# Suffix sums and gate sums of a two-block transformer kernel: fp32 matmuls replaced by pairs of fp32r matmuls on split data

## The chip, the cores and the metric

The kernel runs on one core of one Trainium2 chip. The time is the device time in microseconds of one execution. Three runs of the kernel before gave 1718.21, 1718.66 and 1719.46 us, median 1718.66.

## What is computed

Two transformer blocks over 256 tokens of width 2048, all data fp32. The first block mixes tokens in three ways (12 heads of windowed attention with a sink, 4 heads of gated linear attention, 8 heads of stick-breaking attention), then has a squared-ReLU MLP of width 8192. The second has grouped-query attention in a window, a pooling branch, gates and merges. The change touches two sums of the first block:

```
# stick-breaking attention: sum over later keys
log_1m_beta = where(strict, log_sigmoid(-z), 0)
between     = cumsum(log_1m_beta, reverse=True) - log_1m_beta
w           = where(strict, exp(log_sigmoid(z) + between), 0)
out         = w @ v

# gated linear attention, chunks of 64 tokens
log_gate = max(log_sigmoid(gate_pre) / 16, -1)
b        = cumsum(log_gate)            # within a chunk
q_dec, k_inv, k_end = q * exp(b), k * exp(-b), k * exp(b_last - b)
```

Both are written as products with constant 128x128 matrices of zeros and ones (`mats`): C_SUFFIX (a >= b) and C_ONES for the suffix sums, C_TRI and C_REV (within a chunk, up to and after a token) for the gate sums.

## The kernel before

Weights stream from memory in pieces of 256 rows by 512 columns; one piece is a slot (or sub). For each slot SyncE loads `raw`, ScalarE copies it to `w_hi` (fp32r, a shorter format, which rounds), VectorE writes `w_lo = raw - w_hi` (line 1259), and TensorE does three products per operand pair: hi by hi, hi by lo, lo by hi. In the first phase, P1, that is 12 matmuls a slot (`gemm`, line 653), with the activations `X_pair` as the stationary operand and the weights as the moving one. ScalarE and VectorE make the halves three slots ahead of TensorE; four pieces of halves and eight of raw weights fit on chip. Blocks of columns take eight slots; the block in slots 48 to 55 has 272 columns, the others of this stretch 512.

Everything else is in named stages, each at a slot of its phase (the STAGES list, `stage(phase, slot, name, P=, A=, D=, G=)`, which counts the semaphore steps that it takes on TensorE, ScalarE, VectorE and GpSimd). Each engine walks through the slots in order (`walk`, line 500): at slot s TensorE does the matmuls of s, ScalarE and VectorE the halves of s + 3, and after that each does its part of the stages of slot s. Before its part of a stage an engine calls `enter` (line 492), which waits until all engines have done all stages that stand before it in the list:

```python
def enter(eng, name, turn=None):
    phase, before_, _ = BASE[name]
    for e in "PADG":
        if before_[e]:
            n = before_[e]
            eng.wait_ge(SIDE[e], ...)
```

The stick-breaking heads go in two groups of four, 0 and 1. sb_Z: scores on TensorE, two copies to SBUF on ScalarE. sb_P: exponential and logarithm on ScalarE. sb_Q (line 1401): VectorE makes `soft`, 128 x 1536, and masks it. sb_S (line 877): five fp32 matmuls of the matrices with `soft` (three of 512 columns, two of 256); then VectorE subtracts and masks (lines 1413 to 1420). sb_W: exponential on ScalarE, line 1135. sb_V: 12 matmuls with 64 columns of values, copied out by VectorE, line 1424. The stages in0 to in10 move a finished block of products out of PSUM on ScalarE (line 1097), and free its bank for the second block behind it.

The gated attention: gla_A and gla_B make the gate's argument, gla_K (VectorE) the log gates `lg`, 128 x 2 x 384. gla_C: four fp32 matmuls of C_TRI and C_REV with `lg` (384 columns each, lines 914 and 915), eight small fp32 ones (line 919), then ScalarE's exponentials. swa_N takes mean squares of the windowed attention's result on ScalarE, with a root on GpSimd. gla_D (VectorE, last line 1435) multiplies q and k, gla_E transposes them on TensorE (line 623), and so on to gla_O. In the trace each fp32 matmul shows as two instructions.

The stage "vectors" at slot 9 makes some small constants on VectorE.

Of the kernel before, what the change touches and what calls it, by code (L numbers as in the profile page):

```python
# [27 lines left out]
P = 128  # L28
D_MODEL = 2048
TOK = 256  # L30
NT = TOK // P
KC = D_MODEL // P
NW = 512
# [31 lines left out]
V_MIX, V_MLP, V_PRE, V_GAIN, V_C, V_POOL, V_FIN, V_MER, V_COLS = 0, 16, 32, 48, 64, 80, 88, 104, 136  # L65

C_ID, C_TRI, C_REV, C_SUFFIX, C_STRICT, C_NEG, C_ONES, C_CHUNK = range(8)


def constants():  # L70
# [104 lines left out]
def stage(phase, slot, name, P=0, A=0, D=0, G=0):  # L175
    STAGES.append((phase, slot, name, dict(P=P, A=A, D=D, G=G)))
# [25 lines left out]
stage("P1", 43, "sb_Z0", P=1, A=2)  # L202
stage("P1", 44, "sb_P0", A=2)
stage("P1", 46, "sb_Q0", D=2)
stage("P1", 49, "sb_S0", P=1, D=2)
stage("P1", 50, "in5", A=1)
stage("P1", 52, "sb_W0", A=1)
stage("P1", 54, "sb_V0", P=1, D=1)
stage("P1", 55, "sb_Z1", P=1, A=2)
stage("P1", 56, "sb_P1", A=2)  # L210
stage("P1", 57, "gla_ones", G=1)
stage("P1", 58, "sb_Q1", D=2)
stage("P1", 60, "in6", A=1)
stage("P1", 61, "sb_S1", P=1, D=2)
stage("P1", 63, "sb_W1", A=1)
stage("P1", 64, "in7", A=1)
stage("P1", 65, "sb_V1", P=1, D=1)
stage("P1", 66, "gla_A", P=1, A=1)
stage("P1", 66, "sb_N", A=2, G=2)
stage("P1", 68, "gla_B", P=1, A=3)  # L220
stage("P1", 69, "sb_M", D=1)
stage("P1", 70, "gla_K", D=2)
stage("P1", 71, "in8", A=1)
stage("P1", 73, "gla_C", P=1, A=1)
stage("P1", 75, "swa_N", A=2, G=2)
stage("P1", 75, "gla_D", D=1)
stage("P1", 77, "gla_E", P=1, A=1, D=1)
# [106 lines left out]
def done(e, name, turn=None):  # L334
    return step(e, name, BASE[name][2][e], turn)


def program(nc, t, out):
    f32, f32r = mybir.dt.float32, mybir.dt.float32r
    ACT = mybir.ActivationFunctionType  # L340
    AX = mybir.AxisListType
    ctx = ExitStack()
    with ctx:
# [9 lines left out]
        def put(name, at, shape, dt=f32):  # L353
            size = (4 * int(np.prod(shape[1:])) + 31) // 32 * 32
            assert at + size <= room - 64, (name, at, size, room)
            return nc.alloc_sbuf_tensor_at(name, shape, dt, offset=base + at), at + size

        raw, at = put("raw", 0, [P, RAW, SUB, NW])
        w_hi, at = put("w_hi", at, [P, SPLIT, SUB, NW], f32r)
        w_lo, at = put("w_lo", at, [P, SPLIT, SUB, NW], f32r)  # L360
        x, at = put("x_res", at, [P, NT, D_MODEL])
        X_AT = at
        x_pair, at = put("X_pair", at, [P, KC, 2, TOK], f32r)
        x_hi, x_lo = x_pair[:, :, 0, :], x_pair[:, :, 1, :]
        mats, at = put("mats", at, [P, 8, P])
        vecs, at = put("vecs_sb", at, [P, V_COLS])
        stat, at = put("stat", at, [P, 96])
        small, at = put("small", at, [P, 96])
        half, at = put("minus_half", at, [P, 8])
        cs, at = put("c_silu", at, [P, KC])  # L370
        ada_v, at = put("ada_v", at, [P, 2, KC])
        pre_g, at = put("pre_gain", at, [P, KC])
        sinks, at = put("sinks", at, [P, SWA_HEADS + Q_HEADS2])
        nsinks, at = put("nsinks", at, [P, SWA_HEADS + Q_HEADS2])
        AR = at
        Y_AT = (room - 64 - 32 * KB) // 32 * 32
        y_pair, _ = put("Y_pair", Y_AT, [P, KC, 2, TOK], f32r)
# [3 lines left out]
        swa, at = put("swa", AR, [P, NT, SWA_END])  # L381
        sbp, at = put("sbp", at, [P, NT, 3 * SB_W])
        gla, at = put("gla", at, [P, NT, SB_AT - SWA_END])
        M1_AT = at
        bias1, at = put("bias1", M1_AT, [P, SWA_HEADS, TOK])
        HT_AT = at
        heads_T, at = put("heads_T", HT_AT, [HD, 16, TOK])
        PR_AT = at
        probs, at = put("probs", PR_AT, [P, 1536])
        probs_T, at = put("probs_T", at, [P, 1536])  # L390
        soft, at = put("soft", at, [P, 1536])
        assert at <= room - 64, (at, room)
        onehot, _ = put("onehot_sb", PR_AT, [BUCKET_ROWS, 2, TAB])
        rel, _ = put("rel_sb", PR_AT + 4 * KB, [BUCKET_ROWS, SWA_HEADS + Q_HEADS2])
        tab, _ = put("tab_sb", PR_AT + 8 * KB, [SWA_HEADS, 2, TAB])

        GW = GLA_HEADS * GLA_DK
        GV = GLA_HEADS * GLA_DV
        lg, at = put("log_gate", M1_AT, [P, NT, GW])
        e_dec, at = put("e_dec", at, [P, NT, GW])  # L400
        e_inv, at = put("e_inv", at, [P, NT, GW])
        e_end, at = put("e_end", at, [P, NT, GW])
        assert at <= HT_AT
        qd_T, at = put("qd_T", HT_AT, [GLA_DK, NT, GLA_HEADS, P])
        ki_T, at = put("ki_T", at, [GLA_DK, NT, GLA_HEADS, P])
        sc_T, at = put("sc_T", at, [P, NT, GLA_HEADS, P])
        blr_T, at = put("blr_T", at, [GLA_RANK + 1, TOK])
        gw, at = put("gw_sb", at, [GLA_RANK + 1, GW])
        dec, at = put("decay", at, [GLA_DK, GLA_HEADS, 2 * NT])
        assert at <= PR_AT  # L410
        state, at = put("state", PR_AT, [GLA_DK, 3, GLA_HEADS, GLA_DV])
        k_inv, at = put("k_inv", PR_AT + 9 * KB, [P, NT, GW])

        ada_w, at = put("ada_w", AR, [P, 2, ADA_W])
        hid, at = put("hid", at, [P, NT, NW])
        x_nf, at = put("x_nf", at, [P, NT, NW])
        norm_f, at = put("norm_f", at, [P, D_MODEL])
        acc, at = put("ada_acc", at, [P, ADA_W])
        acc_T, at = put("ada_acc_T", at, [P, ADA_W])
        at = max(at, AR + 48 * KB)  # L420
        ada_sum, at = put("ada_sum", at, [P, QUARTERS * ADA_W // GRP])
        gate_T, _ = put("gate_T", at, [KC, P])
        b_ada, at = put("b_ada", at, [ADA_ROWS, P])
        post, at = put("post_gain", at, [KC, P])
        gate_v, at = put("gate_v", at, [P, KC])
        row, at = put("gate_row", at, [P, D_MODEL])
        assert at <= Y_AT, (at, Y_AT)

        y_n, _ = put("y_n", X_AT, [P, NT, D_MODEL])
        tmp_T, _ = put("tmp_T", X_AT + 16 * KB, [P, 4, NW])  # L430
# [7 lines left out]
        ya, at = put("ya", AR, [P, Q_HEADS2, TOK])  # L438
        v2, at = put("v2", at, [P, NT, KV_HEADS2 * P])
        probs2_T, at = put("probs2_T", AR + 12 * KB, [P, 4, 2, P])  # L440
        ga, at = put("ga", at, [P, 8, TOK])
        yp, _ = put("yp", at, [P, 8, TOK])
        u, at = put("u", at, [P, 8, PAD + TOK + PAD])
        gp, at = put("gp", at, [P, 8, TOK])
        sums, at = put("window_sums", at, [P, 2, 2, PAD + TOK + PAD])
        assert at <= AR + 48 * KB
        pool_edge, _ = put("pool_edge", AR + 10 * KB, [P, 4, 2, PAD])

        sig, at = put("sig", AR, [P, 2, 4, TOK])
        br, _ = put("br", at, [P, 4, TOK])  # L450
        m_hi, at = put("M_hi", AR + 16 * KB, [P, KC, TOK], f32r)
        m_lo, at = put("M_lo", at, [P, KC, TOK], f32r)
        o_sb, _ = put("o_sb", AR, [P, NT, D_MODEL])
        sq, _ = put("sq", X_AT, [P, NT, NW])
# [166 lines left out]
        def _(pe):  # L621
# [169 lines left out]
            def stages(name, i):  # L791
# [85 lines left out]
                elif name[:4] == "sb_S":  # L877

                    pe.wait_ge(const_in, 48)
                    for a in range(2):  # L880
                        nc.tensor.matmul(S[:, a, :], mats[:, C_SUFFIX, :], soft[:, NW * a:NW * (a + 1)],
                                         start=True, stop=False)
                        late = S[:, a, :].rearrange("p (h q) -> p h q", h=2)[:, :, P:TOK]
                        nc.tensor.matmul(late, mats[:, C_ONES, :], soft[:, 2 * NW + TOK * a:2 * NW + TOK * (a + 1)]
                                         .rearrange("p (h q) -> p h q", h=2), start=False, stop=True)
                    nc.tensor.matmul(S[:, 2, :], mats[:, C_SUFFIX, :], soft[:, 2 * NW:3 * NW],
                                     start=True, stop=True).then_inc(pe_side, 1)
                elif name[:4] == "sb_V":
                    for k in range(4):
                        h = 4 * int(name[-1]) + k  # L890
# [20 lines left out]
                elif name == "gla_C":  # L911

                    for tt in range(NT):
                        nc.tensor.matmul(S[:, tt, 0:GW], mats[:, C_TRI, :], lg[:, tt, :], start=True, stop=True)
                        nc.tensor.matmul(S[:, 2 + tt, 0:GW], mats[:, C_REV, :], lg[:, tt, :], start=True, stop=True)
                    for h in range(GLA_HEADS):
                        for tt in range(NT):
                            c_ = GW + 4 * h + 2 * tt
# [81 lines left out]
        def _(act):  # L1000
# [38 lines left out]
            def stages(name, i):  # L1039
# [89 lines left out]
                elif name[:4] == "sb_P":  # L1129

                    nc.scalar.activation(probs_T[:, :], probs_T[:, :], ACT.Exp, scale=-1.0).then_inc(act_side, 1)
                    act.wait_ge(act_side, step("A", name, 1))
                    nc.scalar.activation(soft[:, :], probs_T[:, :], ACT.Ln, bias=1.0).then_inc(act_side, 1)
                elif name[:4] == "sb_W":
                    nc.scalar.activation(probs_T[:, :], probs[:, :], ACT.Exp).then_inc(act_side, 1)
                elif name == "gla_A":
# [117 lines left out]
        def _(dve):  # L1254
# [68 lines left out]
            def stages(name, i):  # L1323
# [86 lines left out]
                elif name[:4] == "sb_S":  # L1410
# [7 lines left out]
                    b = probs[:, 1024:1536].rearrange("p (h q) -> p h q", h=4)  # L1418
                    nc.vector.tensor_tensor(a, a, neg, ALU.add)
                    nc.vector.tensor_tensor(b, b, neg, ALU.add).then_inc(dve_side, 1)  # L1420
                elif name[:4] == "sb_V":
                    dve.wait_ge(pe_side, done("P", name))
                    c = 4 * HD * int(name[-1])
# [102 lines left out]
                elif name == "vectors":  # L1526

                    dve.wait_ge(const_in, 48)
                    nc.vector.tensor_scalar(nsinks[:, :], sinks[:, :], -1.0, None, ALU.mult)
                    nc.vector.tensor_tensor(pre_g[:, :], vecs[:, V_PRE:V_PRE + KC], vecs[:, V_FIN:V_FIN + KC],  # L1530
                                            ALU.mult).then_inc(dve_side, 1)
# [234 lines left out]
```

## Time and profile before

| | us | share | instructions |
|---|---|---|---|
| profiled execution | 1718.24 | | |
| its span | 1716.4 | 100% | 27560 |
| TensorE matmul | 1696.1 | 99% | 10425 |
| TensorE weight load | 1507.0 | 88% | 10425 |
| VectorE | 1104.2 | 64% | 1115 |
| ScalarE | 824.6 | 48% | 1072 |
| GpSimd | 55.0 | 3% | 53 |

The time is the execution's own; the span goes from its first to its last instruction. Shares are busy time over the span. Matmuls are pipelined, so their shown durations overlap: the distance between starts says what one costs in a stream. The mean granted TensorE clock was 0.998 of full speed.

### The profile page before, as it was taken

The page shows a single profiled execution, that of the slowest core. Times are in us where ns is not written, and L with a number is a line of the kernel's source. Part 1 is how long each engine was busy: PE and PEld are TensorE (multiplying, and loading weights), DVE is VectorE, ACT ScalarE, POOL GpSimd, SP SyncE. Part 2 cuts the span into 40 slices and gives each one's busy share as a digit, 9 for nine tenths or more (in the row PEclk, how much of TensorE's full clock was granted, in tenths as well). Part 3 has the DMA queues.
Part 4 walks back from the last instruction along what each step waited for, and adds up shares of the span by engine and source line. Part 5 has one row for each costly group of instructions (what it writes and reads, how often), then busy time and mean ns, then how long its engine had stood idle before and what let it go on. Part 6 is the DMA issues. An engine that isn't in the chain of part 4 may idle for free.

```text
span 1716.4 us, 27560 instructions
## 1 busy us (share of the span) xinstructions
PE 1696.1 (99%) x10425; PEld 1507.0 (88%) x10425; DVE 1104.2 (64%) x1115; ACT 824.6 (48%) x1072; POOL 55.0 (3%) x53
## 2 busy tenths in 40 slices
PE   9999999999999999999999999999999999999998
PEld 6888888789998999889988998799989988888886
DVE  4544545555777677777777777765565566757654
ACT  6455554544444544454444444444434444444443
POOL 1000000000000000000000000000000001101100
PEclk9999999999999999999999999999999999999999
DMA  8642644466777777777777787656455656565662
GB/s 305 192 147 63 199 148 149 140 210 222 278 271 264 252 250 273 261 258 276 253 249 265 268 283 260 227 172 202 156 163 169 189 180 195 183 190 177 197 207 87
DMA packets 170689, 361.59 MB, mean 211 GB/s; under 512 B 10907, under 2 KB 15579, under 8 KB 170336
## 3 DMA queue, kind: packets, MB, share of 16 engines
q1 hardware_dynamic: 168272, 352.24, 61.9%
q0 software_dynamic: 2032, 7.56, 1.3%
q8 instruction: 73, 1.20, 0.3%
q10 hardware_dynamic: 288, 0.39, 0.1%
q14 instruction: 24, 0.20, 0.0%
HBM read 358.00 MB, written 2.15 MB: 210 GB/s over the span
## 4 chain that ended last, share of the span: by engine, by line
PE 83%; DVE 1%; issue 0%; DVEq 0%; POOL 0%; ACT 0%; ACTq 0%
PE G L636 32%; PE G L653 30%; PE S L667 5%; PE G L667 5%; PE G L670 3%; PE S L670 3%; PE S L653 3%; PE S L623 1%; PE G L642 1%; PE S L986 0%; PE S L979 0%; PE S L966 0%; PE S L940 0%; PE S L951 0%; PE S L955 0%
## 5 line engine op out<-in xcount | busy, mean ns | idle before, releaser
L1259 DVE TENSOR_TENSOR w_lo<-raw,w_hi 128x1024 fp32r<-128x1024 f32 (+2 forms) x576 | 708.1, 1245 | 467.6 <-ACT w_hi L1009 466.2
L1009 ACT ACTIVATE w_hi<-raw 128x1024 fp32r<-128x1024 f32 (+2 forms) x576 | 594.8, 1046 | 586.9 <-PE G L653 230.6
L653 PE MATMUL G<-w_hi,X_pair 128*128 128x512 f32 (+2 forms) x1984 | 607.7, 385 | 2.1 <-DVE w_lo L1259 1.3
L636 PE MATMUL G<-Y_pair,w_hi 128*128 128x256 f32 x3136 | 554.7, 280 | 0.0
L636 PEld LDWEIGHTS G<-Y_pair,w_hi 128*128 128x128 f32 x3136 | 478.4, 188 | 2.8 <-issue 1.9
L653 PEld LDWEIGHTS G<-w_hi,X_pair 128*128 128x128 f32 x1984 | 368.8, 188 | 79.3 <-issue 5.7
L636 PE MATMUL G<-Y_pair,w_lo 128*128 128x256 f32 x1568 | 437.1, 279 | 0.0
L653 PE MATMUL G<-w_lo,X_pair 128*128 128x512 f32 (+2 forms) x992 | 379.6, 383 | 0.0
L636 PEld LDWEIGHTS G<-Y_pair,w_lo 128*128 128x128 f32 x1568 | 294.8, 188 | 0.0
L653 PEld LDWEIGHTS G<-w_lo,X_pair 128*128 128x128 f32 x992 | 186.5, 188 | 35.6 <-issue 0.5
L1272 DVE SCALAR_TENSOR_TENSOR ada_acc<-ada_w,c_silu,ada_acc 128x768 f32<-128x768 f32 x120 | 121.3, 1011 | 0.0
L667 PE MATMUL S<-Y_pair,w_hi 128*128 128x512 f32 x256 | 88.9, 390 | 0.0
L667 PE MATMUL G<-Y_pair,w_hi 128*128 128x512 f32 x256 | 88.9, 390 | 0.0
L670 PE MATMUL S<-Y_pair,w_lo 128*128 128x256 f32 x256 | 72.2, 282 | 0.0
L670 PE MATMUL G<-Y_pair,w_lo 128*128 128x256 f32 x256 | 72.2, 282 | 0.0
L667 PEld LDWEIGHTS G<-Y_pair,w_hi 128*128 128x128 f32 x256 | 48.0, 188 | 10.1
L667 PEld LDWEIGHTS S<-Y_pair,w_hi 128*128 128x128 f32 x256 | 48.0, 188 | 10.1
L670 PEld LDWEIGHTS S<-Y_pair,w_lo 128*128 128x128 f32 x256 | 48.4, 189 | 0.0
L670 PEld LDWEIGHTS G<-Y_pair,w_lo 128*128 128x128 f32 x256 | 48.4, 189 | 0.0
L667 PE MATMUL S<-X_pair,w_hi 128*128 128x512 f32 x128 | 44.6, 391 | 0.0
L667 PE MATMUL G<-X_pair,w_hi 128*128 128x512 f32 x128 | 44.5, 391 | 0.0
L1192 ACT ACTIVATE S<-x_res 128x512 f32<-128x512 f32 x32 | 19.3, 603 | 43.9 <-DVE x_res L1505 43.4
(292 smaller groups left out, 1269.5 us busy)
## 6 DMA issues: line engine op xcount, KB each, us to landing
raw<-in_w_in SPq DMA_DIRECT2D x144, 512.0 KB, 4.4
raw<-in_w_mlp_in SPq DMA_DIRECT2D x128, 512.0 KB, 5.3
raw<-in_w_mlp_out SPq DMA_DIRECT2D x128, 512.0 KB, 6.5
ada_w<-in_w_ada SPq DMA_DIRECT2D x64, 768.0 KB, 4.8
raw<-in_w_out SPq DMA_DIRECT2D x64, 512.0 KB, 4.3
raw<-in_w_merge SPq DMA_DIRECT2D x64, 512.0 KB, 4.1
raw<-in_w_branch_attn SPq DMA_DIRECT2D x16, 512.0 KB, 4.3
raw<-in_w_branch_pool SPq DMA_DIRECT2D x16, 512.0 KB, 5.7
```

The costliest lines, as they stand in the source:

```text
L623: return nc.tensor.transpose(out_, in_, ident)
L636: ins = nc.tensor.matmul(G[:, bank, j // 2, TOK * (j % 2):TOK * (j % 2 + 1)], w[:, s % SPLIT, c, cut], a[:, c0 + c, :], start=first and c ...
L642: ins = nc.tensor.matmul(G[:, bank, 1, TOK * tt:TOK * (tt + 1)], a[:, c0 + c, P * tt:P * (tt + 1)], w[:, s % SPLIT, c, P * turned:NW], sta ...
L653: ins = nc.tensor.matmul(token_bank(bank, tt)[:, 0:n], a[:, c0 + c, tok], w[:, s % SPLIT, c, 0:n], start=first and c == 0 and k == 0, stop ...
L667: nc.tensor.matmul(bank, w_hi[:, s % SPLIT, c, cut], both[:, c0 + c, :, :].rearrange("p a q -> p (a q)"), start=first and c == 0, stop=Fal ...
L670: ins = nc.tensor.matmul(bank[:, 0:TOK], w_lo[:, s % SPLIT, c, cut], both[:, c0 + c, 0, :], start=False, stop=last and c == SUB - 1, skip_ ...
L1009: nc.scalar.activation(w_hi[:, s % SPLIT, :, 0:n], raw[:, k, :, 0:n], ACT.Copy).then_inc(hi_ready, 1)
L1192: nc.scalar.activation(junk, src, ACT.Square, scale=D_MODEL ** -0.5, accum_out=stat[:, c:c + 1]).then_inc(act_side, 1)
L1259: nc.vector.tensor_tensor(w_lo[:, s % SPLIT, :, 0:n], raw[:, k, :, 0:n], w_hi[:, s % SPLIT, :, 0:n], ALU.subtract).then_inc(lo_ready, 1)
L1272: nc.vector.scalar_tensor_tensor(a, w, cs[:, v:v + 1], a, ALU.mult, ALU.add).then_inc(ada_free, 1)
```

## The change

The data of the sums are split as the weights are: a half `hi` (rounded copy on ScalarE) and a half `lo = data - hi` (VectorE), both fp32r. The matrices are copied once to fp32r, in which zeros and ones are exact. Each fp32 matmul becomes two fp32r matmuls that add into the same bank, the matrix with `hi` and with `lo`. The two new kinds of stages, sb_H0 and sb_H1 behind sb_Q and gla_H behind gla_K, make the halves. `soft_hi` lies on `probs_T`, `soft_lo` on `soft`, `lg_hi` and `lg_lo` on the places of `e_dec` and `e_inv`, all free at that time. Most stages between slots 49 and 73 move one slot later, and in5 now stands before sb_S0 in the list. The eight small matmuls of gla_C stay fp32.

```diff
-stage("P1", 49, "sb_S0", P=1, D=2)
+stage("P1", 47, "sb_H0", A=1, D=1)
 stage("P1", 50, "in5", A=1)
-stage("P1", 52, "sb_W0", A=1)
-stage("P1", 54, "sb_V0", P=1, D=1)
+stage("P1", 50, "sb_S0", P=1, D=2)
+stage("P1", 53, "sb_W0", A=1)
+stage("P1", 55, "sb_V0", P=1, D=1)
 stage("P1", 55, "sb_Z1", P=1, A=2)
 stage("P1", 56, "sb_P1", A=2)
 stage("P1", 57, "gla_ones", G=1)
 stage("P1", 58, "sb_Q1", D=2)
+stage("P1", 59, "sb_H1", A=1, D=1)
 stage("P1", 60, "in6", A=1)
-stage("P1", 61, "sb_S1", P=1, D=2)
-stage("P1", 63, "sb_W1", A=1)
+stage("P1", 62, "sb_S1", P=1, D=2)
 stage("P1", 64, "in7", A=1)
-stage("P1", 65, "sb_V1", P=1, D=1)
+stage("P1", 64, "sb_W1", A=1)
+stage("P1", 66, "sb_V1", P=1, D=1)
 stage("P1", 66, "gla_A", P=1, A=1)
 stage("P1", 66, "sb_N", A=2, G=2)
 stage("P1", 68, "gla_B", P=1, A=3)
 stage("P1", 69, "sb_M", D=1)
 stage("P1", 70, "gla_K", D=2)
 stage("P1", 71, "in8", A=1)
-stage("P1", 73, "gla_C", P=1, A=1)
+stage("P1", 72, "gla_H", A=1, D=1)
+stage("P1", 74, "gla_C", P=1, A=1)
...
                 elif name[:4] == "sb_S":
...
-                        nc.tensor.matmul(S[:, a, :], mats[:, C_SUFFIX, :], soft[:, NW * a:NW * (a + 1)],
-                                         start=True, stop=False)
                         late = S[:, a, :].rearrange("p (h q) -> p h q", h=2)[:, :, P:TOK]
-                        nc.tensor.matmul(late, mats[:, C_ONES, :], soft[:, 2 * NW + TOK * a:2 * NW + TOK * (a + 1)]
-                                         .rearrange("p (h q) -> p h q", h=2), start=False, stop=True)
...
+                        for half_ in (soft_hi, soft_lo):
+                            nc.tensor.matmul(S[:, a, :], sum_m[:, M_SUFFIX, :], half_[:, NW * a:NW * (a + 1)],
+                                             start=half_ is soft_hi, stop=False, skip_group_check=True)
+                        for half_ in (soft_hi, soft_lo):
+                            nc.tensor.matmul(late, sum_m[:, M_ONES, :], half_[:, 2 * NW + TOK * a:2 * NW + TOK * (a + 1)]
+                                             .rearrange("p (h q) -> p h q", h=2), start=False, stop=half_ is soft_lo,
+                                             skip_group_check=True)
...
                 elif name == "gla_C":
...
-                        nc.tensor.matmul(S[:, tt, 0:GW], mats[:, C_TRI, :], lg[:, tt, :], start=True, stop=True)
-                        nc.tensor.matmul(S[:, 2 + tt, 0:GW], mats[:, C_REV, :], lg[:, tt, :], start=True, stop=True)
+                        for bank, m in ((tt, M_TRI), (2 + tt, M_REV)):
+                            for half_ in (lg_hi, lg_lo):
+                                nc.tensor.matmul(S[:, bank, 0:GW], sum_m[:, m, :], half_[:, tt, :],
+                                                 start=half_ is lg_hi, stop=half_ is lg_lo, skip_group_check=True)
...
+                elif name[:4] == "sb_H":
+                    act.wait_ge(dve_side, done("D", name.replace("H", "Q")))
+                    nc.scalar.activation(soft_hi[:, :], soft[:, :], ACT.Copy).then_inc(act_side, 1)
+                elif name == "gla_H":
+                    act.wait_ge(dve_side, done("D", "gla_K"))
+                    nc.scalar.activation(lg_hi[:, :, :], lg[:, :, :], ACT.Copy).then_inc(act_side, 1)
...
+                elif name[:4] == "sb_H":
+                    dve.wait_ge(act_side, done("A", name))
+                    nc.vector.tensor_tensor(soft_lo[:, :], soft[:, :], soft_hi[:, :], ALU.subtract).then_inc(dve_side, 1)
+                elif name == "gla_H":
+                    dve.wait_ge(act_side, done("A", name))
+                    nc.vector.tensor_tensor(lg_lo[:, :, :], lg[:, :, :], lg_hi[:, :, :], ALU.subtract).then_inc(dve_side, 1)
...
                 elif name == "vectors":
 
                     dve.wait_ge(const_in, 48)
+                    nc.vector.tensor_copy(sum_m[:, M_TRI:M_SUFFIX + 1, :], mats[:, C_TRI:C_SUFFIX + 1, :])
+                    nc.vector.tensor_copy(sum_m[:, M_ONES, :], mats[:, C_ONES, :])
```

## Rows read from the trace of the kernel before

**Rows 1.** Waits of TensorE, whole span: us in total, times, longest

```profile
PE S L623 <- DVE y_n L1347: 2.0, 1, 2.0
```

**Rows 2.** Chain that ended last, 120 to 310 us: start, us, what

```profile
265.69 1.92 PE S L623 x16
267.62 5.48 PE G L653 x24
```

**Rows 3.** TensorE's timeline around sb_S0: start, us, operation, [idle before <- releaser]

```profile
173.36 1.02 PE L881 MATMUL S<-soft,mats 128*128 128x512 f32 x2
...
176.92 0.28 PE L653 MATMUL G<-w_lo,X_pair 128*128 128x272 f32 x1
...
177.30 0.29 PE L653 MATMUL G<-w_lo,X_pair 128*128 128x272 f32 x1
...
185.59 0.41 PE L893 MATMUL S<-sbp,probs_T 128*128 128x64 f32 x2 [0.86 <-issue]
...
188.27 0.37 PE L653 MATMUL G<-w_hi,X_pair 128*128 128x272 f32 x1
...
189.94 0.70 PE L872 MATMUL S<-heads_T 64*128 64x256 f32 x2
```

**Rows 4.** ScalarE's timeline, 155 to 225 us

```profile
167.34 1.73 ACT L1009 ACTIVATE w_hi<-raw 128x544 fp32r<-128x544 f32 x3
...
180.34 1.27 ACT L1097 ACTIVATE sbp<-G,stat 128x512 f32<-128x512 f32 x2 [6.07 <-DVE probs L1420]
...
182.71 1.28 ACT L1135 ACT_TABLE_LOAD   x1
184.01 1.49 ACT L1135 ACTIVATE probs_T<-probs 128x1536 f32<-128x1536 f32 x1
```

**Rows 5.** VectorE's timeline, 155 to 225 us

```profile
171.69 0.68 DVE L1409 TENSOR_TENSOR soft<-soft,mats 128x512 f32<-128x512 f32 x1
172.29 1.99 DVE L1259 TENSOR_TENSOR w_lo<-raw,w_hi 128x544 fp32r<-128x544 f32 x3
177.09 1.75 DVE L1413 TENSOR_TENSOR probs<-probs,S 128x1536 f32<-128x1536 f32 x1 [2.81 <-PE S L886]
```

**Rows 6.** TensorE's timeline around sb_S1 and sb_V1

```profile
209.22 1.02 PE L881 MATMUL S<-soft,mats 128*128 128x512 f32 x2
...
226.18 0.47 PE L653 MATMUL G<-w_hi,X_pair 128*128 128x512 f32 x1
```

**Rows 7.** ScalarE's timeline, in6

```profile
207.36 0.87 ACT L1097 ACTIVATE gla<-G,stat 128x272 f32<-128x272 f32 x2 [2.27 <-DVE soft L1409]
```

**Rows 8.** VectorE's timeline, end of sb_Q1 and sb_V1

```profile
206.51 0.69 DVE L1409 TENSOR_TENSOR soft<-soft,mats 128x512 f32<-128x512 f32 x1
...
226.50 0.69 DVE L1424 COPY sbp<-S 128x512 f32<-128x512 f32 x1 [2.66 <-PE S L897]
```

**Rows 9.** TensorE's timeline, gla_C to gla_E

```profile
250.03 0.81 PE L914 MATMUL S<-log_gate,mats 128*128 128x384 f32 x2
...
252.61 1.44 PE L919 MATMUL S<-mats,log_gate 128*96 128x2 f32 x16
253.92 0.49 PE L653 MATMUL G<-w_hi,X_pair 128*128 128x512 f32 x1
...
265.69 0.28 PE L623 MATMUL S<-mats,gla 128*96 128x128 f32 x1 [0.59 <-DVE gla L1435]
```

**Rows 10.** ScalarE's timeline, 225 to 275 us

```profile
247.25 2.00 ACT L1009 ACTIVATE w_hi<-raw 128x1024 fp32r<-128x1024 f32 x2
...
257.61 2.02 ACT L1009 ACTIVATE w_hi<-raw 128x1024 fp32r<-128x1024 f32 x2
```

**Rows 11.** Windows: us, busy (x instructions) of PE, PEld, DVE, ACT, POOL, granted clock, DMA

```profile
1116.00:1118.00 2.00, 0.63 (x2) 0.00 (x0) 0.59 (x4) 0.05 (x1) 1.03 (x1) 1.00 0.00 0
1118.00:1124.00 6.00, 5.33 (x31) 5.04 (x32) 5.09 (x14) 4.24 (x9) 0.00 (x0) 0.72 0.01 3
```

**Rows 12.** TensorE's timeline, stage h2_T0

```profile
1118.67 3.53 PE L623 MATMUL S<-mats,y_n 128*128 128x128 f32 x16 [2.04 <-DVE y_n L1347]
```

More of the change, by code:

```diff
@@ L67 @@
 C_ID, C_TRI, C_REV, C_SUFFIX, C_STRICT, C_NEG, C_ONES, C_CHUNK = range(8)
+M_TRI, M_REV, M_SUFFIX, M_ONES = range(4)
 def constants():
@@ L389, in program @@
         probs, at = put("probs", PR_AT, [P, 1536])
+        soft_hi, _ = put("soft_hi", at, [P, 1536], f32r)
         probs_T, at = put("probs_T", at, [P, 1536])
+        soft_lo, _ = put("soft_lo", at, [P, 1536], f32r)
         soft, at = put("soft", at, [P, 1536])
+        sum_m, at = put("sum_mats", at, [P, 4, P], f32r)
         assert at <= room - 64, (at, room)
@@ L399, in program @@
         lg, at = put("log_gate", M1_AT, [P, NT, GW])
+        lg_hi, _ = put("log_gate_hi", at, [P, NT, GW], f32r)
         e_dec, at = put("e_dec", at, [P, NT, GW])
+        lg_lo, _ = put("log_gate_lo", at, [P, NT, GW], f32r)
         e_inv, at = put("e_inv", at, [P, NT, GW])
@@ L880, in stages @@
                     for a in range(2):
-                        nc.tensor.matmul(S[:, a, :], mats[:, C_SUFFIX, :], soft[:, NW * a:NW * (a + 1)],
-                                         start=True, stop=False)
                         late = S[:, a, :].rearrange("p (h q) -> p h q", h=2)[:, :, P:TOK]
-                        nc.tensor.matmul(late, mats[:, C_ONES, :], soft[:, 2 * NW + TOK * a:2 * NW + TOK * (a + 1)]
-                                         .rearrange("p (h q) -> p h q", h=2), start=False, stop=True)
-                    nc.tensor.matmul(S[:, 2, :], mats[:, C_SUFFIX, :], soft[:, 2 * NW:3 * NW],
-                                     start=True, stop=True).then_inc(pe_side, 1)
+                        for half_ in (soft_hi, soft_lo):
[5 more added lines that the diff above has]
+                                             skip_group_check=True)
+                    for half_ in (soft_hi, soft_lo):
+                        ins = nc.tensor.matmul(S[:, 2, :], sum_m[:, M_SUFFIX, :], half_[:, 2 * NW:3 * NW],
+                                               start=half_ is soft_hi, stop=half_ is soft_lo, skip_group_check=True)
+                    ins.then_inc(pe_side, 1)
                 elif name[:4] == "sb_V":
```

## The prediction

> **What bounds the kernel now.** I first read who TensorE waits for over the whole span [rows 1]. The longest entry is 2.0 us of some 1716, so TensorE's own queue sets the time, and an edit counts by what it does there: the work it removes, and the idle time it makes or ends. Near the change another engine leads at one place: VectorE's stage gla_D ends and releases TensorE's gla_E, 16 transposes [rows 9]; from there the chain that ended last stays on TensorE [rows 2]. Then I read the timelines around the three changed sums: TensorE, ScalarE and VectorE for the first suffix sum [rows 3 to 5], the second [rows 6 to 8], the gate sums [rows 9, 10]. A slot is one step of weight work, 12 matmuls; the narrow block has 272 columns in slots 48 to 55.
>
> **Price of the two forms on TensorE.** Starts are what counts, not the durations shown, which overlap. One fp32 suffix stage holds TensorE from 173.36 to 176.92 minus one ordinary pitch, 3.43 us [rows 3]. In the new form it is six matmuls of 512 columns and four of 256. The weight matmuls have exactly that form: 24 in 5.48 us, so 0.228 each at 512 columns and 2.74 a slot [rows 2]; at 272 columns three in 0.38, so 0.125 [rows 3], and I take 256 at the same. Sum 6 x 0.228 + 4 x 0.125 = 1.87 us: 1.56 saved per stage, two stages. The gate sums take 252.61 - 250.03 = 2.58 us [rows 9]. New: eight of 384 columns; between 0.125 and 0.228 in proportion that is 0.173, so 1.38 us: 1.20 saved. In all 4.3 us of TensorE work go. Bounds: above, no saving at all (the operands of 0/1 stationary and split moving data are not in the trace together); below, 384 columns at the 272 price, another 0.4. I take the pitch of the weight matmuls, whose form is the same.
>
> **Price of the halves.** Every stage starts with a wait for all stages before it in the list, on all engines. So the stages are one serial chain, and a new stage lengthens it. sb_H copies 1536 columns on ScalarE; sb_W does as many from the same memory in 1.49 us [rows 4]. It then subtracts 1536 on VectorE, 1.75 as for L1413 [rows 5]. gla_H has half the columns. The copies of the matrices in stage "vectors" (512 columns in all) cost less than L1413's 1.75 on VectorE; the three slots that w_lo is made ahead, 8 us, hide them, and without that cover they would cost at most 1.75. I take nothing. No DMA moves, and SP's loads wait for w_lo seven slots back, so they are not reached.
>
> **First suffix sum.** VectorE ends sb_Q0 at 171.69 + 0.68 = 172.37 [rows 5]. ScalarE, which waits in sb_H0 instead of going on with slot 51's weights, copies from 172.5 to 174.0. VectorE subtracts to 175.8. ScalarE makes the three narrow copies of slots 51 to 53 meanwhile (1.73, [rows 4]), which fit before 175.8. But in5 now stands ahead of sb_S0 in the list, and so sb_S0 waits for it too: 175.8 + 0.16 (207.20 to 207.36 in [rows 7, 8]) + 1.27 [rows 4] = 177.25, and with 0.15 to get TensorE going 177.4. TensorE now does slot 50 first (12 x 0.125 = 1.5; its w_lo, the first of the three in [rows 5], is there at 173.0, before 173.36): it is ready at 173.36 + 1.50 = 174.86. **New idle: 2.5 us.** The sum ends at 179.27. Slots 51 to 55 (7.5) bring TensorE to 186.8. The chain: VectorE's part of sb_S0 took from 177.09 to about 180.2, 3.1 us [rows 4, 5], so it ends at 182.6; ScalarE then does slot 56's wide copy to 183.5, a table load of 1.28 and the exponential 1.49 [rows 4], done 186.3. So sb_V0 is not waited for, and the old idle before it (0.86 shown, 1.0 by pitches, plus 0.27 in slot 54 for w_lo) goes. But sb_V0 and sb_Z1 now stand in one slot with no weight work between. sb_Z1 waits for VectorE's copy of sb_V0's result: 0.32 after the last matmul until it starts, 0.69 for it, 0.2 back [rows 6, 8]. **New idle: 1.2 us.** sb_V0 takes 188.27 - 185.59 = 2.68 [rows 3], so sb_Z1 starts at 186.8 + 2.7 + 1.2 = 190.7, against 189.94 [rows 3]: 0.75 later than before, although 1.56 of work is gone.
>
> **Second suffix sum.** Everything is 0.75 later. sb_Q1 ends at 206.51 + 0.69 + 0.75 = 207.95 [rows 8]; copy to 209.6, subtraction to 211.4, in6 (0.87, [rows 7]) to 212.4. TensorE, with slot 62 now first, arrives at 209.22 + 0.75 + 2.74 = 212.7 [rows 6]: ready, with 0.1 to spare. 1.56 gained. Then the same neighbourhood again: sb_V1 and gla_A share slot 66, where slot 66's matmuls stood between them: 1.2 idle, less 0.1 for one switch of form fewer. Shift now 0.75 - 1.56 + 1.2 - 0.1 = 0.3 later.
>
> **Gate sums.** gla_H goes between in8 and gla_C. ScalarE's copies for slots 75 and 76 ran from 247.25 in 2.00 [rows 10]; the half copy (under 1.49) and the subtraction (under 1.75) with waits end before 252, and TensorE comes from slot 74 only at 250.03 + 0.3 + 2.74 = 253.07. Hidden; if not, it would cost one for one. gla_C ends at 253.07 + 1.38 + 1.31 (the 16 small ones, unchanged) = 255.76, 1.84 later than 253.92 [rows 9]. Behind it hangs the chain to gla_E: exponentials, swa_N, POOL's root, gla_D, gla_E. Of it one wide copy drops out (slot 77's, now ahead of gla_C; the two took 2.02 at 257.61, [rows 10]): -1.0. So gla_E starts 0.85 later, at 266.5. TensorE has only three slots between instead of four: 255.76 + 8.22 = 263.98. **New idle: 2.55 us, where 0.8 was (0.59 shown).** The 1.20 saved here disappears in it. What is late next is this chain, and behind gla_E nothing changes.
>
> **Sum.** +0.85 us on the profiled execution's 1718.24 (span 1716.4 and 1.84 around it): 1719.1. The median of the runs is 0.42 above that execution: 1719.5. A difference under 0.2%, 3.4 us, can't be told from none here.
>
> **Clock.** At 1116 to 1118 TensorE was idle for most of the time; its wait was 2.04 us, and when it came back with transposes, the granted clock fell: mean 0.72 over 1118 to 1124, which is (1 - 0.72) x 6 / 0.5 = 3.4 us at 0.5, 1.2 GHz [rows 11]. The 16 transposes there took 3.53 us [rows 12] against 1.92 for the 16 of gla_E [rows 2]. Price of a fall: half of 3.4, 1.7 us. The Trainium skill, "TensorE: Matmul & The Clock Gate", section "HAM oscillation — how this bites in real kernels", says that bursts of matmuls parted by waits come back at half the clock and pay beyond the wait. The trace agrees at this one place. [...] The waits of 0.86 and 0.59 us [rows 3, 9] left the clock at full speed, and by them alone it would be 1719.5.
>
> **Rivals.**
> - Half clock after the new waits. Place: the idle of 2.5 before sb_S0 and of 2.55 before gla_E, the latter followed by transposes as in rows 12. For: both are longer than 2.04. Against: dense weight work stands right ahead of both and behind the first, while at 1116 the work around was thin. One fall: 1719.5 + 1.7 = 1721.2. Both: 1722.9, slower than the bound of 1722.1. It decides from the second fall on.
> - The halves and in5 are out of the way in time, and the work saved is kept: 4.3 and the old idles of 1.27 and 0.8 give 1718.66 - 6.4 = 1712.3. Against it: even with both halves free, sb_S0 would wait for in5 until 175.8 or so. With that, half of the way: 1717.5, no change.
> - The form doesn't do what it says: fp32 speed remains. Then 3.1 of the two suffix stages comes back and of the gates 1.2: 1723.8. Against: L653 is that form.
>
> **Chances.** Forecast 0.50 (its own range 1718.3 to 1720.7, from latencies of 0.1 to 0.3 in four waits). One fall of the clock 0.20, both 0.13. Waits smaller than I count 0.12, half of it past 3.4 us. No gain from the form 0.05. Faster: 0.06. Slower: 0.13 + 0.05, less 0.02 for cases that come out milder: 0.16. Within: 0.78. Range 1716.5 to 1722.9: it takes in both falls and leaves out the full gain and the form without gain.
>
> **What would show it.** Fp32r pairs at S at 0.228 spacing; TensorE idle ahead of sb_S0 by 2.5 with in5 as the last to end; 1.2 before sb_Z1 and before gla_A, both on VectorE's copy; no idle before sb_V0; 2.5 before gla_E, whose start is at 266 to 267. Wrong: gla_E before 265, clock below 1.00 between 170 and 275, or halves longer than 1.8 us.

## The result and the profile after

The changed kernel takes 1722.72 us in the median of 20 runs (1718.83 to 1727.54), the kernel before 1717.89 (1716.81 to 1719.46, 20 runs). The ratio is 1.0027, interval 1.0020 to 1.0033: slower by 4.8 us in the medians. The forecast was 1719.5 with a range of 1716.5 to 1722.9. The time is in the range, 0.2 us below its upper end, but the likeliest case was not what happened: a difference of less than 0.2% had 0.78, and the result is the slower case, which had 0.16. The spread is a finding of its own: 8.7 us between runs, where the kernel before has 2.7. It goes with the clock: the mean granted clock of a run falls from 0.999 in the fastest to 0.994 in the slowest, and 0.005 of 1720 us is 8.6 us.

The profiled execution took 1721.95 us, its span 1720.1 against 1716.4. The page:

```profile
PE 1693.1 (98%) x10425; PEld 1506.8 (88%) x10425; DVE 1109.0 (64%) x1120; ACT 828.1 (48%) x1075; POOL 55.0 (3%) x53
```

TensorE is 3.0 us less busy than before with as many instructions, and still the span is 3.7 longer. The waits of TensorE (us in total, times, longest) name where:

```profile
PE S L892 <- ACT sbp L1113: 2.4, 1, 2.4
PE S L632 <- DVE gla L1463: 2.4, 1, 2.4
PE S L632 <- DVE y_n L1369: 2.0, 1, 2.0
...
PE S L632 <- DVE sbp L1452: 1.1, 1, 1.1
PE S L881 <- DVE sbp L1452: 1.1, 1, 1.1
```

Three of these are new: sb_S0 waits for in5's copy (sbp, ScalarE), gla_A and sb_Z1 for VectorE's copies out of sb_V. A fourth, gla_E's wait for gla_D, was 0.59 before [rows 9]. The two short ones come from the list. Of the twenty stages between slots 49 and 73 only seven move; sb_Z1 and gla_A stay, so sb_V0 now shares slot 55 with sb_Z1, and sb_V1 shares slot 66 with gla_A, with no weight matmuls between. TensorE's timeline around sb_S0, to be held against [rows 3]:

```profile
174.66 0.28 PE L662 MATMUL G<-w_hi,X_pair 128*128 128x272 f32 x1
177.37 0.47 PE L892 MATMUL S<-soft_hi,sum_mats 128*128 128x512 f32 x1 [2.42 <-ACT sbp L1113]
177.68 0.40 PE L892 MATMUL S<-soft_lo,sum_mats 128*128 128x512 f32 x1
177.91 0.28 PE L895 MATMUL S<-soft_hi,sum_mats 128*128 128x256 f32 x1
...
179.30 0.29 PE L662 MATMUL G<-w_hi,X_pair 128*128 128x272 f32 x1
...
186.82 0.33 PE L907 MATMUL S<-sbp,probs_T 128*128 128x64 f32 x2
...
190.69 0.67 PE L881 MATMUL S<-heads_T 64*128 64x256 f32 x2 [1.08 <-DVE sbp L1452]
```

The pairs take 179.30 - 177.37 = 1.93 us where fp32 took 3.43, and sb_Z1 starts at 190.69 where it started at 189.94. Then the part that these rows don't show. The windows after it (us, busy of PE, PEld, DVE, ACT, POOL, granted clock, DMA):

```profile
186.00:190.00 4.00, 3.61 (x32) 3.47 (x31) 2.59 (x3) 2.32 (x3) 0.00 (x0) 1.00 0.87 304
190.00:192.00 2.00, 1.31 (x8) 1.23 (x9) 0.43 (x1) 0.00 (x0) 0.00 (x0) 1.00 0.87 291
192.00:194.00 2.00, 2.00 (x11) 1.74 (x9) 0.00 (x0) 0.00 (x0) 0.00 (x0) 0.66 0.59 211
194.00:196.00 2.00, 2.00 (x6) 1.49 (x5) 0.00 (x0) 1.61 (x2) 0.00 (x0) 0.50 0.00 0
196.00:198.00 2.00, 2.00 (x6) 1.53 (x5) 0.00 (x0) 2.00 (x2) 0.00 (x0) 0.50 0.00 0
198.00:200.00 2.00, 2.00 (x7) 1.52 (x7) 1.23 (x1) 1.98 (x3) 0.00 (x0) 0.63 0.00 0
200.00:202.00 2.00, 2.00 (x10) 1.65 (x9) 0.00 (x0) 1.99 (x2) 0.00 (x0) 1.00 0.71 199
```

The clock is at 0.50, 1.2 GHz, from about 193 to 199. The missing clock (what the stretch lacks to full speed) is (0.34 + 0.50 + 0.50 + 0.37) x 2 = 3.4 us. Before it stood sb_V0, 12 matmuls with 64 columns (thin ones, in what follows), 1.1 us of idle time, and sb_Z1 with 64 rows. Around it, across both waits of 2.4 us and the second short one, the clock stayed up:

```profile
170.00:190.00 20.00, 17.18 (x132) 16.52 (x131) 14.61 (x17) 11.33 (x13) 0.00 (x0) 1.00 0.71 237
202.00:280.00 78.00, 74.53 (x368) 61.97 (x367) 44.25 (x43) 42.93 (x53) 3.27 (x7) 1.00 0.48 156
```

The second suffix sum starts without a wait and takes 1.86 us:

```profile
215.83 0.39 PE L892 MATMUL S<-soft_hi,sum_mats 128*128 128x512 f32 x1
...
217.69 0.40 PE L662 MATMUL G<-w_hi,X_pair 128*128 128x512 f32 x1
```

The gates, beside [rows 9]:

```profile
256.23 0.34 PE L930 MATMUL S<-log_gate_hi,sum_mats 128*128 128x384 f32 x1
...
257.64 1.44 PE L935 MATMUL S<-mats,log_gate 128*96 128x2 f32 x16
258.95 0.47 PE L662 MATMUL G<-w_hi,X_pair 128*128 128x512 f32 x1
...
269.78 0.29 PE L632 MATMUL S<-mats,gla 128*96 128x128 f32 x1 [2.38 <-DVE gla L1463]
```

1.41 us for the pairs instead of 2.58. gla_E starts at 269.78 against 265.69: 4.1 later, 3.4 by the clock and 0.7 by the chain. Of that, 0.4 comes back near 1120 us, where this execution had no fall of the clock and [rows 11] had one: the 16 transposes take 2.14 us instead of 3.53, and a wait of 0.96 for Y_pair follows in their place.

```profile
1122.74 2.14 PE L632 MATMUL S<-mats,y_n 128*128 128x128 f32 x16 [2.04 <-DVE y_n L1369]
1125.85 0.50 PE L645 MATMUL G<-Y_pair,w_hi 128*128 128x256 f32 x2 [0.96 <-DVE Y_pair L1380]
```

### The profile page after: what moved, and what is told of

Its sections match the earlier page's. It is cut to its first block, busy times and chain, and to the rows that moved or that the text cites. A ratio compares the mean times of both kernels' runs of the same rounds, so it can differ in the third digit from the quotient of the medians.

```text
span 1720.1 us, 27580 instructions
## 1 busy us (share of the span) xinstructions
PE 1693.1 (98%) x10425; PEld 1506.8 (88%) x10425; DVE 1109.0 (64%) x1120; ACT 828.1 (48%) x1075; POOL 55.0 (3%) x53
## 4 chain that ended last, share of the span: by engine, by line
PE 83%; DVE 1%; issue 0%; ACT 0%; DVEq 0%; POOL 0%; ACTq 0%
PE G L645 32%; PE G L662 29%; PE S L676 5%; PE G L676 5%; PE G L679 3%; PE S L679 3%; PE S L662 3%; PE S L632 1%; PE G L651 1%; PE S L1002 0%; PE S L995 0%; PE S L982 0%; PE S L956 0%; PE S L967 0%; PE S L971 0%
```

## The experiments

Theory: the change saves 4.3 us of TensorE work; the chain of stages turns that into a net loss of about 0.9; and the rest is the clock, which falls behind stretches in which TensorE does little. Rivals: the waits or the pairs cost more by themselves; the halves are what costs; or the long waits, as the prediction had it, not the thin stretches, drop the clock.

### Filling the waits

The kernels do fp32 matmuls into a free bank before they enter the stage, and nobody reads the result: one before sb_Z1 and gla_A, two before sb_S0 and gla_E, there behind a wait for the bank's last reader. An entry of FILL has the stage, the number of matmuls, the bank and the stages to wait for:

```diff
+FILL = [('sb_Z1', 1, 0, []), ('gla_A', 1, 0, []), ('sb_S0', 2, 0, [('A', 'sb_P0'), ('D', 'sb_Q0')]), ('gla_E', 2, 3, [('A', 'gla_C')])]
...
+                for fill_name, fill_n, fill_bank, fill_after in FILL:
+                    if name == fill_name:
+                        for e_, st_ in fill_after:
+                            pe.wait_ge(SIDE[e_], done(e_, st_))
+                        for _ in range(fill_n):
+                            nc.tensor.matmul(S[:, fill_bank, :], mats[:, C_ONES, :],
+                                             mats[:, C_TRI:C_TRI + 4, :].rearrange("p a b -> p (a b)"), start=True, stop=True)
                 enter(pe, name, i)
```

The other kernels with filling have fewer entries in FILL. Their line numbers are up to 10 higher than in the changed kernel.

All four:

> The changed kernel with idle TensorE time filled: before it enters sb_S0 and gla_E it does two, before sb_Z1 and gla_A one fp32 matmul of 512 columns (0.85 us each) whose result nobody reads. Theory A (the new waits cost 0.85 us net, and the rest of the loss is the granted clock falling behind the thin stretches): no fall between 170 and 275 us, time 1718.7 to 1719.5, highest run within 2 us of the lowest. Rival B (the loss sits in the waits or in the new form itself, not in the clock): 1722.7 stays. Rival C (the filling comes late in its stage and delays it): up to 3 us more than 1722.7.

Measured 1719.34 (1718.33 to 1720.38, 11 runs), ratio to before 1.0009 (1.0000 to 1.0018). Adding work made the kernel 3.4 us faster, and the spread is 2.0 us. Theory A holds, B and C fall. By the medians the chain's price is some 1.3 us beside the 1717.99 of before. The profiled execution puts it at 0.76: gla_E starts at 266.45, where it started at 265.69.

```profile
266.45 1.92 PE S L633 x16
```

Only the two short waits behind sb_V:

> Filling only the two waits of 1.1 us before sb_Z1 and gla_A, one matmul each. Theory A1 (the falls start behind the thin stretches of 64-column matmuls and the wait after them, as in the profile, where the clock was 0.50 from 193 to 199 us): about 1719, as with all four filled. Rival A2 (the falls come from the two longer waits of 2.4 us before sb_S0 and gla_E): little changes, 1721 to 1723.

Measured 1719.56 (1718.11 to 1722.21, 11 runs), ratio 1.0014 (1.0005 to 1.0023). The median is that of all filled, but four of the 11 runs lie at 1720.7 or more, at a mean clock of 0.996 or 0.997. A1 for the most part. Where the clock fell in those four isn't shown; the open long waits are the likely place. In the profiled execution both stand open, and the clock is 1.00 from 170 to 275 us:

```profile
PE S L901 <- ACT sbp L1122: 2.4, 1, 2.4
PE S L633 <- DVE gla L1472: 2.4, 1, 2.4
```

There gla_E starts at 266.22, 0.53 later than before: this is the changed kernel's chain with the clock held.

Only the two long ones:

> The changed kernel with only the two waits of 2.4 us before sb_S0 and gla_E filled, two matmuls each; the thin stretches of sb_V and the waits behind them stay. With the two short waits filled instead, the time fell from 1722.7 to 1719.6 but single runs still reached 1722.2. Theory A1 (most falls start behind the thin stretches of sb_V): this kernel keeps them, median 1720.5 to 1722, single runs at 1723 or more. Rival A2 (the long waits are the main cause): 1719.5, as with all filled.

Measured 1723.15 (1718.38 to 1726.40, 10 runs), ratio 1.0029 (1.0019 to 1.0038): as slow as the changed kernel, and above the 1720.5 to 1722 expected. Eight of ten runs lie at 1721.6 or more, two at 1718.4. The windows of its profiled execution, with a fall behind each of the two sb_V:

```profile
186.00:196.00 10.00, 8.92 (x52) 7.84 (x51) 3.02 (x3) 4.47 (x5) 0.00 (x0) 0.84 0.61 211
...
228.00:238.00 10.00, 8.92 (x41) 7.10 (x40) 3.15 (x3) 3.83 (x7) 0.95 (x2) 0.83 0.41 134
```

The same windows with all four filled:

```profile
186.00:196.00 10.00, 9.83 (x61) 8.22 (x60) 3.02 (x3) 4.67 (x5) 0.00 (x0) 1.00 0.63 220
...
228.00:238.00 10.00, 9.83 (x40) 6.67 (x40) 3.05 (x3) 5.07 (x9) 0.95 (x2) 1.00 0.48 151
```

The stretch is the same but for 0.9 us of work in the middle. A2, which was the prediction's place for the fall, is refuted as the main cause. One thing stays open: the filling ends the idle time and puts a matmul of full width between two thin stretches, both at once, so these runs don't tell whether the wait or the thin work around it is what drops the clock.

### The slots alone

The kernel before with the changed list of slots, without sb_H and gla_H and with fp32 sums:

```diff
-stage("P1", 49, "sb_S0", P=1, D=2)
 stage("P1", 50, "in5", A=1)
+stage("P1", 50, "sb_S0", P=1, D=2)
...
-stage("P1", 73, "gla_C", P=1, A=1)
+stage("P1", 74, "gla_C", P=1, A=1)
```

> The kernel before with the changed kernel's list of slots, without the stages that make halves, sums in fp32 as before. By the chain: sb_S0 waits 0.7 us for in5, sb_Z1 and gla_A 1.2 each, gla_E starts 3.3 us later than in the kernel before. So 1721.2 with the clock held, and 2 to 4 us more where it falls: 1723 to 1725. Rival (the slots are free and the halves are what costs): 1718.

Measured 1725.94 (1725.20 to 1727.67, 5 runs), ratio 1.0049 (1.0035 to 1.0063). That is 0.9 above the expected 1723 to 1725; the rival's 1718 falls. The new order is slower than the whole change, without any pair or half in it. With the waits before sb_Z1, gla_A and gla_E filled as above:

> The kernel with only the slots changed (fp32 sums, no halves) and the waits before sb_Z1, gla_A and gla_E filled. Unfilled it took 1725.9, and its profile shows 10.2 us at half clock. If 3.3 us of its loss are the chain and the rest the clock, 1720.8 to 1721.5 here, with single runs close together. Rival (the waits themselves cost all of it): 1725.9 stays.

Measured 1721.25 (1720.58 to 1723.65, 11 runs), ratio 1.0019 (1.0010 to 1.0028). So the order costs 3.2 us by the chain (1718.04 before, beside it) and 4.7 by the clock. With the waits filled in both, the kernel with pairs takes 1719.34 and this one 1721.25: in these slots the pairs give back 1.9 of the 3.2, which leaves the 1.3 above. (This kernel has no filling before sb_S0, where its wait is 0.5.) The profile of the unfilled one has (1 - 0.75) x 10 + (1 - 0.76) x 4 + (1 - 0.88) x 14 = 5.1 us of missing clock in these windows:

```profile
186.00:196.00 10.00, 8.92 (x47) 7.81 (x47) 3.02 (x3) 2.77 (x4) 0.00 (x0) 0.75 0.62 213
196.00:200.00 4.00, 4.00 (x15) 3.22 (x14) 1.02 (x1) 4.00 (x4) 0.00 (x0) 0.76 0.00 0
...
266.00:280.00 14.00, 11.64 (x53) 9.65 (x52) 10.06 (x11) 6.78 (x10) 0.93 (x2) 0.88 0.39 120
```

The last of them holds the fall that the prediction expected: behind the wait of 2.4 us before gla_E and in its transposes. So that place can bring one; in the three other profiled executions with that wait open (the changed kernel, the short waits filled, the gate sums alone) it did not.

### The gate sums alone

The suffix sums and their slots as before, gla_H at 72 and gla_C at 74:

> Only the gate sums in the new form, with gla_H at 72 and gla_C at 74 as in the changed kernel; suffix sums and their slots as in the kernel before. By the chain behind gla_C: gla_E waits 2.5 us and starts 0.55 us later than in the kernel before, though 1.2 us of TensorE work is gone: 1718.4 with the clock held; a single long wait, followed by transposes, gives a fall in some runs: 1718.4 to 1719.5. Rival (the saved work is kept): 1716.8.

Measured 1718.07 (1717.72 to 1719.45, 11 runs), ratio 1.0003 (0.9994 to 1.0012), before beside it 1717.58. No difference can be told; the rival's 1716.8 lies below every run. The profile shows gla_E's wait of 2.4 us and the clock at 1.00 until the end:

```profile
PE S L630 <- DVE gla L1456: 2.4, 1, 2.4
```

```profile
260.00:280.00 20.00, 17.62 (x95) 14.85 (x94) 12.55 (x13) 9.90 (x14) 0.93 (x2) 1.00 0.43 132
```

By the median this long wait, with dense work ahead of it, costs nothing by the clock here. The 1.2 us of saved work show up nowhere.

### in5 behind sb_S0

```diff
-stage("P1", 50, "in5", A=1)
 stage("P1", 50, "sb_S0", P=1, D=2)
+stage("P1", 51, "in5", A=1)
```

> The changed kernel with in5 behind sb_S0 (slot 51) and the waits filled, one matmul before sb_S0, sb_Z1 and gla_A, two before gla_E. Question: did in5 ahead of sb_S0 cost its 1.4 us? If only the waits at sb_S0 counted: 1718.0. By the chain it is moved, not removed: in5 then stands between sb_S0 and sb_W0, ScalarE makes the halves of slots 55 and 56 behind it, sb_W0 ends at 187.1 and sb_V0 starts 0.3 to 0.4 later than it did: 1719.4 to 1719.8, the same as with all waits filled.

Measured 1719.63 (1719.03 to 1725.18, 12 runs), ratio 1.0019 (1.0010 to 1.0028). The median is as expected. The wait moved: the profile has 1.3 us before sb_V0 (line 916 there).

```profile
PE S L916 <- issue: 1.3, 1, 1.3
```

Eight runs lie between 1719.0 and 1720.7 with a mean clock of 0.998 or 0.999, four between 1724.3 and 1725.2 with 0.995. So the four are slower by the clock. sb_V0 now had an unfilled wait ahead of it, which fits the thin-stretch theory, but there is no trace of any of the four, so where the clock fell isn't shown.

### Slots with room

```diff
-stage("P1", 50, "in5", A=1)
-stage("P1", 50, "sb_S0", P=1, D=2)
+stage("P1", 51, "sb_S0", P=1, D=2)
+stage("P1", 52, "in5", A=1)
 stage("P1", 53, "sb_W0", A=1)
-stage("P1", 55, "sb_V0", P=1, D=1)
-stage("P1", 55, "sb_Z1", P=1, A=2)
...
+stage("P1", 56, "sb_V0", P=1, D=1)
+stage("P1", 57, "in6", A=1)
+stage("P1", 57, "sb_Z1", P=1, A=2)
...
+stage("P1", 64, "sb_S1", P=1, D=2)
...
+stage("P1", 67, "sb_V1", P=1, D=1)
+stage("P1", 68, "gla_A", P=1, A=1)
...
+stage("P1", 76, "gla_C", P=1, A=1)
...
+stage("P1", 80, "gla_E", P=1, A=1, D=1)
```

> The changed kernel with another list of slots: sb_S0 at 51 ahead of in5, sb_V0 and sb_Z1 a slot apart (56, 57), sb_V1 and gla_A (67, 68), gla_C at 76 and gla_E at 80 with four slots between. If the work saved is real and only the waits ate it: none of the four waits, gain 4.3 of work plus about 2 of old idle: 1712.0 to 1713.5, and no fall of the clock in this stretch. Rival (the chain of stages is too long by two more slots and the end of the phase waits for it): 1716 to 1720.

Measured 1715.46 (1714.29 to 1716.38, 11 runs), ratio 0.9982 (0.9973 to 0.9991): a gain, but 2 us short of what was expected. All four waits are gone, and the clock is 1.00 from 170 to 290 us. Others came, for the halves of the weights: 2.6 us in two waits. The timeline of TensorE at slot 56:

```profile
185.51 0.29 PE L662 MATMUL G<-w_hi,X_pair 128*128 128x272 f32 x1
186.77 0.47 PE L662 MATMUL G<-w_hi,X_pair 128*128 128x512 f32 x1 [0.98 <-DVE w_lo L1281]
```

First step, in5 from 52 to 53:

> The respaced kernel with in5 one slot later (53), behind the halves of slot 56. In the trace of the respaced kernel TensorE waited 1.0 us for w_lo of slot 56, since ScalarE made in5 first. If that is all, 1714.4 to 1714.8 against 1715.5. Rival (sb_W0, now later, makes sb_V0 wait instead): 1715.5.

Measured 1713.44 (1712.71 to 1715.11, 11 runs), ratio 0.9976 (0.9967 to 0.9985): 1.0 further than expected, 0.4 of which is the kernel before, whose runs beside it are that much faster (1717.58 instead of 1717.99). Beside it the same slots without halves, in fp32:

> The same list of slots without the stages for halves and with all sums in fp32 as before: what the form alone is worth where no wait hides it. By the prediction's prices 2 x 1.56 + 1.20 = 4.3 us more than the same slots with pairs: 1718.9. Rival (the halves on ScalarE and VectorE cost what the matmuls save): the same time as with pairs, 1714.6.

Measured 1715.75 (1715.23 to 1716.20, 11 runs), ratio 0.9988 (0.9979 to 0.9997). The form is worth 2.3 us here, not 4.3: neither theory nor rival. TensorE, ScalarE and VectorE of the kernel with pairs, around slot 51, show where 1.8 of it went:

```profile
174.80 0.28 PE L662 MATMUL G<-w_hi,X_pair 128*128 128x272 f32 x1
176.68 0.39 PE L662 MATMUL G<-w_hi,X_pair 128*128 128x272 f32 x1 [1.59 <-DVE w_lo L1281]
```

```profile
172.61 1.49 ACT L1152 ACTIVATE soft_hi<-soft 128x1536 fp32r<-128x1536 f32 x1 [3.46 <-DVE soft L1431]
174.00 2.28 ACT L1025 ACTIVATE w_hi<-raw 128x544 fp32r<-128x544 f32 x4
```

```profile
174.23 1.76 DVE L1445 TENSOR_TENSOR soft_lo<-soft,soft_hi 128x1536 fp32r<-128x1536 f32 x1 [1.15 <-ACT soft_hi L1152]
175.91 2.63 DVE L1281 TENSOR_TENSOR w_lo<-raw,w_hi 128x544 fp32r<-128x544 f32 x4
```

ScalarE sat idle 3.46 us in sb_H0's wait although slot 51's weights could have been copied, and their w_lo came behind soft_lo. Second step, `stage("P1", 48, "sb_H0")` instead of 47, which puts slot 51's halves ahead of it:

> The respaced kernel with sb_H0 at slot 48 instead of 47. In the trace of the respaced kernel the form gained only 2.3 us over fp32 in the same slots, not 4.3, and TensorE waited from 174.9 to 176.7 us for w_lo of slot 51, which ScalarE and VectorE made only after the halves of soft. If that wait is what the form's gain lost, it goes and the time is 1711.5 to 1711.9 (1713.4 less 1.8). Rival (the waiting moves on to sb_S0 itself or to slot 52): 1713.

Measured 1711.09 (1710.93 to 1712.08, 5 runs), ratio 0.9961 (0.9948 to 0.9974): 6.95 us faster than before and 11.6 than the changed kernel in their medians. Some 2 of the 7 us come from the slots alone, as the fp32 kernel shows. In TensorE's timeline the sum follows the weights without a gap:

```profile
176.18 0.29 PE L662 MATMUL G<-w_hi,X_pair 128*128 128x272 f32 x1
176.31 0.39 PE L892 MATMUL S<-soft_hi,sum_mats 128*128 128x512 f32 x1
176.53 0.40 PE L892 MATMUL S<-soft_lo,sum_mats 128*128 128x512 f32 x1
...
178.16 0.29 PE L662 MATMUL G<-w_hi,X_pair 128*128 128x272 f32 x1
```

By the ratios the pairs are worth 0.9988 - 0.9961 = 0.0027, 4.6 us, against fp32 in slots that differ only in sb_H0, which fp32 hasn't. With the two intervals that is some 2 to 7 us, so it agrees with the prediction's 4.3 and doesn't measure it closely.

## Why the prediction was right or wrong

- **Price of the two forms.** 1.87 us forecast, 1.93 and 1.86 (215.83 to 217.69) measured; gates 1.38 and 1.41. Right, and taking the pitch of the weight matmuls was the right choice of row.
- **Price of the halves.** 1.49 and 1.76 us in sb_H0 as forecast; they lengthen the chain as forecast. The prediction saw that ScalarE's copies for slots 51 to 53 come later and rightly took them as hidden; it gave no price to VectorE's w_lo of the same slots, which comes behind soft_lo. In the changed kernel that too hides in sb_S0's wait; it cost 1.8 us as soon as that wait was gone.
- **First suffix sum.** Start of sb_S0 177.4 forecast, 177.37 measured; sb_V0 not waited for; sb_Z1 at 190.7, measured 190.69. Right.
- **Second suffix sum.** Right once the 3.4 us are taken off: sb_S1 at 215.83 - 3.4 = 212.4 (212.7 forecast), the wait of 1.1 before gla_A.
- **Gate sums.** Wait of 2.4 us (2.55 forecast), gla_E 0.7 late without the clock (0.85 forecast). Right, and confirmed by the gates alone.
- **Sum.** +0.85 us by the chain. With the waits filled the kernel stands at +1.3, the interval 0 to 3.1 us; gla_E starts at 266.45 there and at 266.22 with the short waits filled, where 266.5 was forecast. Right.
- **Clock.** The prediction's own sign of being wrong came, a clock below 1.00 between 170 and 275 us, and gla_E started at 269.8, not at 266 to 267. What failed is the weighing of the rival: "the idle of 2.5 before sb_S0 and of 2.55 before gla_E", one fall at 0.20 and both at 0.13, against 0.50 for none. Its price per fall was 1.7 us, its place the two longest waits. The runs show that no fall is the rare case (two of the 20 runs, 1718.83 and 1719.08, have a mean clock of 0.999, and three more, 1719.8 to 1721.0, have 0.998, which the kernel before has with its one fall near 1118), that the main place is sb_V with the 1.1 us behind it, at both groups, and that one fall there can last 6.8 us and cost 3.4. The rival's time for two falls, 1722.9, is close to the measured 1722.7, but from another place, and the range reached the measured time only by these two falls. That it did is luck. The prediction had the two short waits in its own sum and asked of them only what they last.
- **The other rivals.** The full gain did not come: sb_S0 waited for in5, as was said against it. That the form does nothing is refuted by 1.93 us against 3.43.

The Trainium skill, "TensorE: Matmul & The Clock Gate", section "HAM oscillation — how this bites in real kernels", which the prediction named beside its rival, has short bursts of matmuls parted by waits for DMA of some 3 to 5 us, each burst starting at half the clock. The traces agree that the clock comes back at half (0.50 from 193 to 199 us). But those waits are longer than any here, so the section says nothing of what a wait of 2.4 us would do. Here 2.4 us before sb_S0 left the clock at full speed in the changed kernel's profile, and 1.1 us between thin matmuls did not.

## What to carry to other kernels

Work taken from the busiest engine is a gain only where the next thing it needs is ready earlier too; count the chain of stages to the next entry, and when a stage is added, also what its waiting engine would have made meanwhile. Two stages that depend on each other should not share a slot with nothing between. Judge a wait on TensorE with the work around it: behind matmuls of few columns even a microsecond of waiting cost three more by the clock here, and putting work that nobody needs into the wait is a cheap test of that.

## What had not been expected of the hardware

The clock fell more often around thin matmuls with a short wait (1.1 us behind 2.7 us of 64-column matmuls, at both groups in one profiled execution) than at the waits of 2.4 us behind dense ones: with only the short waits filled the median was 1719.56, with only the long ones 1723.15. A fall lasted 3.4 us in some executions and 6.8 in others, and TensorE was busy all through the long ones. And such falls are a matter of chance from run to run, so they show as spread: 8.7 us between 20 runs with the waits open, 2.0 between 11 with them filled, 2.1 and 2.4 between 11 with them removed. fp32r matmuls with 384 columns came at 0.176 us from start to start, near the line between the 0.125 and 0.228 of 272 and 512.
